# A chunked RWKV-7 scan rewritten: unrolled over 25 tiles, in 64x64 quarters of TensorE

## The reference, cut to what matters

```python
def _wkv_step(S, xs):
    r_t, w_t, k_t, v_t, kk_t, a_t = xs
    sa = jnp.einsum('zbhvk,zbhk->zbhv', S, -kk_t)
    S = (S * w_t[..., None, :]
         + sa[..., :, None] * (kk_t * a_t)[..., None, :]
         + v_t[..., :, None] * k_t[..., None, :])
    o = jnp.einsum('zbhvk,zbhk->zbhv', S, r_t)
    return S, o
```

## Time and profile before

| what | us |
|---|---|
| median of 3 runs (3643.79 to 3665.93) | 3649.31 |
| the profiled execution | 3657.51 |
| its span, first to last instruction | 3655.7 |
| the scan in it, 1058.5 to 2189.7 | 1131.3 |

### The profile page before, as it was taken

One profiled execution on the slowest core, in us unless ns is written; L12 is line 12 of the kernel. 1 busy time (PEld: TensorE's weight loads), 2 busy tenths in 40 slices (PEclk: granted clock), 3 DMA queues, 4 the chain that ended last, 5 costly groups with the idle time before them and its releaser, 6 DMA issues. The chain is left out here.

```text
span 3655.7 us, 75267 instructions
## 1 busy us (share of the span) xinstructions
PE 3072.8 (84%) x31095; PEld 2605.7 (71%) x31095; DVE 1815.6 (50%) x3080; ACT 1056.3 (29%) x1765; POOL 890.9 (24%) x572
## 2 busy tenths in 40 slices
PE   2799779999967888888888864969999994999996
PEld 1688665555546777777777763759999984999995
DVE  5243463344435777777777754642233334333324
ACT  2111102233324554454445531121121112212121
POOL 3111140000022322222223203633232313223232
PEclk9999895688878999999999986979999996999998
DMA  4121210000010000010001003442222205222210
GB/s 144 50 73 52 84 63 21 12 12 11 9 47 20 26 27 26 27 32 27 26 26 32 14 19 133 155 147 71 67 62 64 69 0 162 58 69 63 63 46 34
DMA packets 180004, 196.22 MB, mean 54 GB/s; under 512 B 13067, under 2 KB 140427, under 8 KB 179723
## 3 DMA queue, kind: packets, MB, share of 16 engines
q1 hardware_dynamic: 179756, 192.58, 17.0%
HBM read 148.59 MB, written 43.96 MB: 53 GB/s over the span
## 5 line engine op out<-in xcount | busy, mean ns | idle before, releaser
L2150 POOL TENSOR_TENSOR ff_w_lo<-ff_w,ff_w_hi 128x1024 fp32r<-128x1024 f32 x132 | 313.5, 2398 | 755.7 <-ACT ff_w_hi L2177 565.9
L2310 PE MATMUL ff_gu<-ff_x_hi,ff_w_hi 128*128 128x384 f32 x1408 | 472.4, 336 | 2.8 <-DVE ff_x_lo L2230 2.8
L2310 PE MATMUL ff_gu<-ff_x_lo,ff_w_hi 128*128 128x384 f32 x1408 | 472.0, 335 | 0.0
L2310 PE MATMUL ff_gu<-ff_x_hi,ff_w_lo 128*128 128x384 f32 x1408 | 471.9, 335 | 0.0
L2241 DVE SCALAR_TENSOR_TENSOR ff_th<-ff_th,ff_gu 128x384 f32<-128x384 f32 x88 | 48.9, 555 | 581.8 <-ACT ff_th L2190 581.8
L1390 ACT ACTIVATE sc_XTd<-sc_XT 64x512 f32<-64x512 f32 x300 | 188.1, 627 | 342.1 <-DVE sc_XT L1487 337.5
L2310 PEld LDWEIGHTS ff_gu<-ff_x_hi,ff_w_hi 128*128 128x128 f32 x1408 | 265.7, 189 | 4.4 <-DVE ff_x_lo L2230 3.6
L2310 PEld LDWEIGHTS ff_gu<-ff_x_hi,ff_w_lo 128*128 128x128 f32 x1408 | 265.5, 189 | 0.8
L2310 PEld LDWEIGHTS ff_gu<-ff_x_lo,ff_w_hi 128*128 128x128 f32 x1408 | 265.5, 189 | 0.0
L2255 DVE TENSOR_TENSOR ff_y<-ff_dn,ff_y 128x512 f32<-128x512 f32 x264 | 180.4, 690 | 136.5 <-PE ff_dn L2323 136.2
L935 PE MATMUL at_S<-at_kT,at_qT 64*128 64x512 f32 x320 | 210.2, 777 | 0.8 <-DVE at_qT L843 0.8
(11 more groups left out here) (275 smaller groups left out, 6503.5 us busy)
## 6 DMA issues: line engine op xcount, KB each, us to landing
ff_w<-in_w_ffn_in SPq DMA_DIRECT2D x88, 512.0 KB, 5.0
ff_w<-in_w_ffn_out SPq DMA_DIRECT2D x44, 512.0 KB, 3.7
sc_rk<-scratch_rkv SPq DMA_DIRECT2D x24, 512.0 KB, 3.4
scratch_rkv<-co_tm SPq DMA_DIRECT2D x12, 768.0 KB, 3.9
pj_x<-in_x SPq DMA_DIRECT2D x13, 512.0 KB, 3.6
co_w<-in_w_in SPq DMA_DIRECT2D x13, 512.0 KB, 4.8
scratch_scan<-sc_out SPq DMA_DIRECT2D x24, 260.0 KB, 2.1
mo_sc<-scratch_scan SPq DMA_DIRECT2D x24, 260.0 KB, 2.9
```

Source lines behind the costliest of these rows:

```text
L2150: nc.gpsimd.tensor_tensor(w_lo[:, q, x, :], w[:, q, x, :], w_hi[:, q, x, :].bitcast(F32), ALU.subtract).then_inc(done, 1)
L2310: last = nc.tensor.matmul(gu[:, g, m, 0:GRP], ww[:, q, m, k * P:(k + 1) * P], xx[:, k, g * GRP:(g + 1) * GRP], start=(j == 0), stop=(j == ...
```

## The change

The scan is written anew. There is one row of 25 tiles: q = 0 is the meta tile, then the tiles of the backward (odd q) and forward (even q) stream in turn. There is no loop: `program` writes out 27 windows, and window w holds the prep of tile w, the levels of tile w - 1 and the back of tile w - 2. The order inside a window puts the back into the first third.

Heads and chunks lie otherwise on the chip: the partitions hold one chunk's 64 tokens for two halves of the heads, so every block of 64x64 is one quarter of TensorE's array (64 rows, 64 columns). Products of the levels, the grams, D_V, solve and state run over the four quarters in turn (`QUARTERS`), with two PSUM banks side by side. The block-diagonal copies are gone: XT is no longer updated by a product but X is transposed in each level (four transposes, a copy by ScalarE). The first product "a0" takes the masked keys directly; GpSimd adds the identity to X after it. Halving and shifting of tanh move to a fourth exponential constant (`count`, for the decay) and to ScalarE (for the gate). The state of each chunk is kept in its own buffer of a ring, with a zero and a meta state to start from, so nothing is cleared at a sequence's end. Keys and queries of the state are two separate products; emit (48 matmuls) now includes the queries and its result is copied by ScalarE. SP issues eight loads, two stores of the bonus and eight stores of the output per tile. The core of the diff:

```diff
-W_LOGIT, A_LOGIT, CUM, CHUNK_SUM, T_K, T_R, T_B, T_D = range(8)
...
+TILES = NT + NT + 1
...
+PREP = ("logits", "square", "sums", "kd", "exps", "keys", "tilde", "turn0", "bonus", "turn1", "gram0", "gram1", "dv")
+LEVEL = ("a0", "t0") + tuple(f"{x}{l}" for l in range(1, LEVELS) for x in "yxt")
+BACK = ("keys0", "solve0", "state0", "keys1", "solve1", "state1", "emit")
...
+    for kind, names, first, last in (("prep", PREP, 0.02, 0.93), ("level", LEVEL, 0.0, 0.98), ("back", BACK, 0.01, 0.34)):
+        for k, name in enumerate(names):
+            at.append((first + (last - first) * k / len(names), kind, name))
...
+        QUARTERS = ((0, 0), (1, 1), (0, 1), (1, 0))
...
+            for w in range(TILES + 2):
+                for kind, name in scan_order():
+                    if kind == "prep" and w < TILES:
+                        prep(w, name)
+                    if kind == "level" and 0 <= w - 1 < TILES:
+                        level(w - 1, name[0], int(name[1]))
+                    if kind == "back" and 0 <= w - 2 and name in back_stages(w - 2):
+                        back(w - 2, name)
...
+                    if x == "a":
+                        pool.wait_ge(lp_read, q * PER_LP + 1)
+                        xs = X[:, :, :, :].rearrange("p a u c -> p (a u) c")
+                        nc.gpsimd.tensor_tensor(xs, xs, eye[:, :].unsqueeze(1).broadcast_to([P, RH, CHUNK]), ALU.add).then_inc(x_first, 1)
...
+                    if x == "t":
+                        act.wait_ge(tp_full, q * LEVELS + l + 1)
+                        to = XF[:, q % 2] if l == LEVELS - 1 else XT[:, :, :, :]
+                        nc.scalar.activation(to.rearrange("p a e t -> p (a e t)"), tp[:, :], ACT.Copy).then_inc(tp_read, 1)
...
+                    if x == "y":
+                        dve.wait_ge(lp_full, q * PER_LP + 2 * l)
+                        nc.vector.tensor_tensor(Y[:, :, :, :], pair, mask, ALU.mult).then_inc(lp_read, 1)
+                    if x == "x":
+                        dve.wait_ge(lp_full, q * PER_LP + 2 * l + 1)
+                        nc.vector.tensor_tensor(xs, pair, xs, ALU.add).then_inc(lp_read, 1)
...
+                        pe.wait_ge(lp_read, q * PER_LP + 2 * l - 1)
+                        for n in range(4):
+                            for e, u in QUARTERS:
+                                last = nc.tensor.matmul(lp[half(u), e, n * CHUNK:(n + 1) * CHUNK], AE[half(e), r, u, n, 0, :], X[half(e), n, u, :], start=True, stop=True)
+                        last.then_inc(lp_full, 1)
...
+                    if name == "emit":
...
+                        read(1).then_inc(crossed, 1)
+                        read(0)
+                        inner(0)
+                        pe.wait_ge(crossed, q)
+                        last = inner(1)
```

More of the change, by code:

```diff
@@ L1015, in among @@
[L1015 to L1019, removed]
-def scan_order():
[L1027 to L1032, removed]
+LEVELS = 6
@@ L1097, in scan @@
[L1097 to L1100, removed]
-        const_loaded = sem("sc_const")
[L1103 to L1116, removed]
+        b2 = sb("sc_b2", [P, RW])
+        Bt = sb("sc_Bt", [P, 3, 2, 4, HEAD])
+        Ct = sb("sc_Ct", [P, 3, 2, 4, HEAD])
@@ L1117, in scan @@
+        in_loaded = [sem(f"sc_in{p}") for p in range(2)]
+        v_loaded = [sem(f"sc_v{p}") for p in range(4)]
+        full = [sem(f"sc_full{b}") for b in range(3)]
+        free = [sem(f"sc_free{b}") for b in range(3)]
         kk_raw = sem("sc_kk_raw")
@@ new lines, in state_after, with has_state, back_stages @@
+        def state_after(q, k):
+            s, g = stream(q)
+            return H[:, s, (2 * g + k + 1) % 4]
+        def has_state(q, k):
+            return q == 0 or not (k == 1 and stream(q)[1] in SEQ_END[stream(q)[0]])
+        def back_stages(q):
+            return [name for name in BACK if not (q == 0 and (name[:4] == "keys" or name == "emit"))
+                    and not (name[:5] == "state" and not has_state(q, int(name[5])))]
+        bk_at, h_at = {}, {}
+        for n, at in enumerate((q, name) for q in range(TILES) for name in back_stages(q)):
+            bk_at[at] = n
@@ new lines, in scan, with state_ready, program @@
+        for n, at in enumerate(at for at in bk_at if at[1][:5] == "state"):
+            h_at[at] = n
+        def state_ready(q, k):
+            if q == 0:
+                return 0
+            s, g = stream(q)
+            if k == 1:
+                return h_at[q, "state0"] + 1
+            if g in (0, SEQ_END[s][0] + 1):
+                return 0 if s else h_at[0, "state0" if g == 0 else "state1"] + 1
+            return h_at[q - 2, "state1"] + 1
+        PER_LP = 2 * LEVELS - 1
+        def program(prep, level, back):
+            for w in range(TILES + 2):
[6 more added lines that the diff above has]
+                        back(w - 2, name)
@@ new lines, in _, with wide, prep @@
+                pool.wait_ge(made, 8)
+                pool.wait_ge(const_loaded, 16 * 15)
+                def wide(ap):
+                    return ap.unsqueeze(1).broadcast_to([P, 2, RW // 2])
+                two = lambda ap: ap.rearrange("p (c f) -> p c f", c=2)
+                def prep(q, name):
+                    r, k = (rk[:, q % 2, x].rearrange("p c j f -> p c (j f)") for x in range(2))
+                    if name == "logits":
+                        pool.wait_ge(in_loaded[q % 2], in_count(q))
+                        wait(pool, kt_ok, q)
+                        nc.gpsimd.tensor_tensor(two(kk[:, :]), k, wide(k_k[:, :]), ALU.mult).then_inc(kk_raw, 1)
+                    if name == "square":
@@ L1393, in back @@
-                def back(st, k):
-                    if k not in (0, 3):
-                        return
-                    s = st.s
-                    act.wait_ge(bfull[s], 7 * st.g + k + 1)
-                    wait(act, bvec[s], 7 * st.g)
-                    c = order(k // 3, s)
-                    nc.scalar.activation(RHt[half(c), s, :], bank[64:128, 6 + s, :], ACT.Copy).then_inc(rh_ok[s], 1)
-                program(act, front, back, lambda: None)
+                        wait(act, ct_ok, q)
@@ L1426, in front, with prep @@
+                def prep(q, name):
+                    s, r = direction(q), q % 3
+                    if name == "square":
                         dve.wait_ge(sq_ok, q + 1)
@@ L1702, in mixout @@
+                program(prep, level, back)
 def mixout(nc, d):
```

899 lines of the change are left out of this document (420 added, 479 removed).

## The result

The change makes the kernel faster, by about six tenths of what was forecast: 3496.95 us (median of 4 runs, 3490.87 to 3505.72) against 3648.73 (4 runs, 3643.79 to 3665.93), a ratio of 0.9578 with a 95% interval of 0.954 to 0.9615. The forecast was 3402, its range 3265 to 3560; 152 us are gained where 247 were forecast. The profiled execution took 3497.47 us.

The account below looks back on a forecast made before the run. TensorE and VectorE were taken to share the bound, TensorE the fuller. TensorE's sum (31.4 us) and the chain, 24.3 plus 7.3 of waits, led to 33 us a tile; 2577 + 25 x 33 = 3402 us, range 3265 to 3560.

Parts of the forecast that it names:

- busy sums: Work per tile of the new scan: TensorE 26.4 us (21.5 to 36.1), VectorE 18.6 us.
- the 31 to 36 that were named: Sign for the forecast: a beat of 31 to 36 us between the scan's outputs, given 0.45.
- the tilde products wait behind emit's copy and the exponentials (about 1): Wait on VectorE in a tile's chain of levels, about 1 us of the 7.3 added to the chain.
- rival 4: More gaps let TensorE's clock fall to 1.2 GHz in the scan: 46 us a tile, 3727 us, slower; chance 0.09.
- granted clock over 0.9: Sign for the forecast in the scan's steady part; below 0.75 would have meant rival 4.
- 19 ns a record: TensorE's quarter products of 64 columns: 480 records a tile, 9.1 us (7.0 to 13.9).
- rival 1: Quarters overlap fully and queues interleave well in the scan: 28 us a tile, 3277 us; chance 0.25.
- Rival 2: Quarters gain little and row halves writing one bank don't overlap: 39 us a tile, 3552 us; chance 0.16.
- what stands ahead of the chain: Work and waits on the TensorE and VectorE queues ahead of the levels' steps: 7.3 us on the chain's 24.3.
- Both sums end near 31.5; they don't nest perfectly, so I take 33 us a tile: Scan's tile time: TensorE's sum at 84% busy gives 31.4 us, the chain with its waits 31.6; 33 taken.
- Rival 3: Supply of TensorE instructions in straight code limits the scan: 41 us a tile, 3602 us, close to no change; chance 0.05.
- 2577 + 25 w: Whole kernel's time in us with w us a scan tile; w = 33 gives 3402.

Follow-up runs that it names:

- fifth experiment: Kernel after with exponentials, GpSimd's keys and tilde products moved ahead of emit's output copy, and GpSimd's Rt product made to wait for Ct: 3398.36 us.
- third experiment: Kernel after with ScalarE's exponentials, GpSimd's keys and the tilde products moved ahead of emit's output copy and x2's add: 3481.15 us.
- fourth experiment: Kernel after, its order kept, with spare matmuls that nobody reads filling TensorE's idle time around the first prep transposes: 3493.16 us.
- sixth kernel: Fifth experiment's kernel with cumulative sums ahead of keys1, chunk sums behind x1, ScalarE's gate work behind U's copy, square sum behind y1's mask: 3319.58 us.

## Why the prediction was right in its direction and too large in its size

The direction and the part of the kernel were right, and the time lies in the range. The busy sums came out too: 27.1 us of TensorE a tile against 26.4, 19.7 of VectorE against 18.6. For TensorE this is partly luck: at full clock it is busy 23.6 us (fifth experiment), and the lower clock made up for terms that were too long. The beat did not come out: 37.6 us lie outside the 31 to 36 that were named, 4.6 over the 33. Two steps of the working failed most.

First, "the tilde products wait behind emit's copy and the exponentials (about 1)". The wait was named and mis-sized: it is 4.1 us, from x2's add to y3's mask 6.24 instead of 2.10, some 3 more than counted. By the beat at full clock, moving the exponentials took away 2.3 (35.4, the estimate, to 33.1) and giving VectorE's products the way ahead of GpSimd's another 1.7. The forecast took every VectorE product at 0.69 us. That is what they take in 24 of the 25 tiles of before; what one takes beside GpSimd the first tile shows, in rows that were not read then:

```profile
1085.75 1.76 DVE L1452 TENSOR_TENSOR sc_W<-sc_rk,sc_W 128x512 f32<-128x512 f32 x1
...
1085.18 1.78 POOL L1310 TENSOR_TENSOR sc_av<-sc_kkr,sc_av 128x512 f32<-128x512 f32 x1
```

The Trainium skill says it on its page "SBUF — State Buffer" (section "SBUF: two separate sides"): VectorE's operations with two SBUF inputs and GpSimd share a port that one of them holds for a whole instruction. The rows agree: 1.75 us beside GpSimd, 0.69 without, and VectorE's Y mask, one input of which is PSUM, takes 0.69 us beside GpSimd's bonus product (1468.87 in the fifth experiment).

Second, rival 4, dismissed with "the clock fell after an idle time of 3.7 us, and no gap that I count is over 2". The trace of before already spoke against that: in its straight stretch, granted 0.97 on the whole, the clock fell too, here behind an idle time of 1.64 us (a row of TensorE, then a window):

```profile
1248.54 1.41 PE L1620 MATMUL sc_bank<-sc_Y,sc_XTd 128*64 128x64 f32 x32 [1.64 <-DVE sc_Y L1474]
...
1249.25:1252.66 3.41, 3.41 (x51) 3.25 (x48) 3.37 (x6) 0.48 (x1) 1.27 (x1) 0.50 0.00 0
```

In the kernel after it fell after gaps of 0.80 and 1.00 us close together. The forecast asked of the steady part "granted clock over 0.9"; it was 0.88, in most tiles 0.86 or 0.91. By the estimates above that costs 0.8 to 2.2 us a tile: no slower kernel, but up to half of the missing time. The two steps hang together, since the late tilde products make the gaps ahead of the fall at 1469. They are not one: with that wait gone (fifth experiment) the clock still fell in 14 of 21 tiles, and it held only when waits elsewhere were shortened.

The other terms were off by less, and partly cancelled. VectorE's masks in the steady tile and the next start at 1472.10 (y3), 1477.11, 1484.27, 1487.94 (a0), 1494.06, 1500.40 and 1509.69. So from a0 on a tile takes 6.1, 6.3, 9.3, 5.0, 7.2 and 3.7 us from mask to mask. The forecast's terms, set on the same stretches, give some 4.8, 5.2, 7.6, 4.2, 6.2 and 3.5, together its 31.6 but for rounding. The stretch with the tilde products (9.3) has the largest excess, but the way to y1's mask and the one past the sums ahead of x1 (6.1 and 6.3) were forecast too short as well. Against that a clean level takes 3.74 us, not 4.2, and x2 waits 1.4 us for emit, not 2.4 (from y2's mask to x2's add 3.0 us, where other levels have 1.6).

Quarters were given 19 ns a record between the bounds of 14.5 and 29; 14.7 is measured, so both pairings add up fully and rival 1's premise was right. It did not come to rival 1's time, since TensorE isn't the bound. Emit was given 36 ns, for fear of two row halves on one bank; it takes 25.5 (2.45 us from the first record to x2's, for 96), nearer to a full pair's 29 than to one alone (57). Rival 2 falls with both numbers, and so does the rule of the page "TensorEngine Tiling (Array Packing)" of the Trainium skill as the forecast applied it: no serialisation shows. The rule of the Trainium skill's page "TensorE: Matmul & The Clock Gate", by which no start comes less than 25 ns after another, doesn't hold for the records (14.7 ns); for the kernel's matmuls, of two records each, it is 29 ns and within the rule. The time that it gave, 3477, lies nearer than the forecast, but not for its reason. Two sums are slightly off: the lower bound of TensorE's work adds up to 22.5 us, not 21.5, and what stands ahead of the chain to 7.4, not 7.3; the forecast does not hang on either.

Part of what stands ahead of the chain was named rightly: moving the chunk sums from ahead of x1, on TensorE's list, and the gate's work from ahead of the copy of U, on ScalarE's, gave 2.1 us together. "Both sums end near 31.5; they don't nest perfectly, so I take 33 us a tile" came out only for another kernel, the third experiment's at full clock. For the kernel after with the clock up the estimate is 35.4 to 36.8, so the sum was short even without the clock.

Rival 3 is out for the kernel after: over the 22 intervals no idle time of TensorE put down to issue is over 0.28 us. With the spare records of the fourth experiment there were up to 1.6 us, so the supply of instructions may not lie far off; no run settles that. SP needs 0.65 us a store (eight in 5.24 us), not 0.43, and no engine's wait is put down to a DMA in the steady part. By the formula 2577 + 25 w the measured beat gives 3517 us, 20 more than the run: start and end were a little overrated.

## What to carry to other kernels

In a chain that no engine bounds, price each step by what runs beside it, not by its shortest row: ask which other engine is at work then and where both read SBUF. Then look for the places where a wait of one engine makes TensorE idle (here 0.8 to 2.7 us) and its clock falls, since that can take nearly as much again as the wait: the sixth kernel gained 2.1 us by its waits and 1.8 by its clock. The same code at 1.00 and 0.78 of the clock, in one trace, gives a price without an experiment. The mean clock of a tile alone does not: the kernel after took 37.6 us a tile at 0.86 and at 0.91. And a small clock deficit in a stretch can hide a fall in every tile; ask for it in short stretches. An order of stages is a list for each engine: a cheap step that is moved (an add of 0.69 us) can gain nothing until what was behind it in the list goes first.

## What the runs showed that had not been expected

- VectorE's products of two SBUF tensors (128x512, fp32) take 1.75 us beside a GpSimd product and 0.69 without; GpSimd's take 1.59 to 1.77 instead of 1.27. Run at once they gain nothing: Bt, Ct and GpSimd's three take 5.1 us together (1468.18 to 1473.30 in the kernel after), one after the other they would take 5.2. A wait lets the ones go first that the chain needs.
- Four quarters of 64x64 in turn pass at 14.7 ns a record, one block alone at 57: four quarters overlap fully. Two at a time, the weight loads of 32 records last 0.84 us instead of 0.56.
- One kernel's tiles (exponentials earlier) took 33.1, 34.7, 37.1 and 38.9 us at granted clocks of 1.00, 0.95, 0.86 and 0.78. The fall came after idle times of 0.8 and 1.0 us in the kernel after, of 1.64 in the kernel before.
